# Who makes the low parts of the experts' weights: VectorE alone instead of VectorE and GpSimd in turn

## The reference

```python
for layer in range(2):
    h = h + hybrid_mixer(rmsnorm(h, attn_norm[layer]), w_in[layer], ..., w_out[layer])
    m = rmsnorm(h, ffn_norm[layer])
    h = h + (swiglu(m, ...) if layer == 0 else moe_swiglu(m, router_w[0], wg, wu, wd))
out = rmsnorm(h, final_norm)

def swiglu(h, wg, wu, wd): return (silu(h @ wg) * (h @ wu)) @ wd
# moe: y += gates[:, e:e+1] * swiglu(tokens, wg[e], wu[e], wd[e]), gates 0 but for the top two
```

## Time and profile before

| | |
|---|---|
| median of three runs | 2504.07 us |
| span of the profiled execution (its own time: no other is shown) | 2505.5 us |
| TensorE matmul busy | 2370.1 us, 95% |
| VectorE busy | 1644.0 us, 66% |
| ScalarE busy | 1241.1 us, 50% |
| GpSimd busy | 844.9 us, 34% |

### The profile page before, as it was taken

One profiled execution on the slowest core, in us unless ns is written; L12 is line 12 of the kernel. 1 busy time (PEld: TensorE's weight loads), 2 busy tenths in 40 slices (PEclk: granted clock), 3 DMA queues, 4 the chain that ended last, 5 costly groups with the idle time before them and its releaser, 6 DMA issues.

```text
span 2505.5 us, 30578 instructions
## 1 busy us (share of the span) xinstructions
PE 2370.1 (95%) x10817; PEld 1921.7 (77%) x10817; DVE 1644.0 (66%) x1608; ACT 1241.1 (50%) x1506; POOL 844.9 (34%) x354
## 2 busy tenths in 40 slices
PE   7999999999999999999999999997989889889887
PEld 6888887888888888888788878885667667667665
DVE  3457566655565655656536667666887787877877
ACT  4445444544444444444544544354566556556555
POOL 1212121121222122222112221123666666665664
PEclk9999999999999999999999999997999999999998
DMA  6454554556655555655454455542777877877877
GB/s 222 148 173 147 170 168 147 187 171 200 194 189 186 190 195 185 200 185 186 163 163 160 151 168 168 168 168 99 271 268 259 277 254 263 273 251 265 274 261 251
DMA packets 256824, 502.38 MB, mean 201 GB/s; under 512 B 13972, under 2 KB 14072, under 8 KB 256248
## 3 DMA queue, kind: packets, MB, share of 16 engines
q1 hardware_dynamic: 250368, 501.25, 60.4%
q10 hardware_dynamic: 6392, 0.25, 0.1%
HBM read 499.37 MB, written 2.10 MB: 200 GB/s over the span
## 4 chain that ended last, share of the span: by engine, by line
PE 77%; issue 7%; POOL 6%; DVE 6%; ACT 3%; DMA 0%; POOLq 0%; ACTq 0%; DVEq 0%; SPq 0%
PE acc L1303 19%; PE acc L1305 19%; PE acc L1304 19%; POOL w_lo L486 6%; PE acc L1576 4%; PE acc L1577 4%; PE acc L1578 4%; PE X L1565 2%; ACT w_hi L526 2%; DVE w_lo L810 2%; PE X L1411 1%; PE acc L1637 1%; PE X L1320 0%; PE acc L1638 0%; PE X L1331 0%
## 5 line engine op out<-in xcount | busy, mean ns | idle before, releaser
L486 POOL TENSOR_TENSOR w_lo<-raw,w_hi 128x1024 fp32r<-128x1024 f32 x331 | 830.0, 2510 | 1627.5 <-ACT w_hi L526 1176.3
L526 ACT ACTIVATE w_hi<-raw 128x1024 fp32r<-128x1024 f32 x939 | 985.4, 1059 | 754.1 <-PE acc L1305 558.0
L810 DVE TENSOR_TENSOR w_lo<-raw,w_hi 128x1024 fp32r<-128x1024 f32 x608 | 933.1, 1543 | 609.8 <-ACT w_hi L526 609.4
L1303 PE MATMUL acc<-w_hi,a_hi 128*128 128x512 f32 x1600 | 632.9, 396 | 7.7 <-POOL w_lo L486 3.7
L1305 PE MATMUL acc<-w_hi,a_lo 128*128 128x512 f32 x1600 | 625.8, 391 | 0.0
L1304 PE MATMUL acc<-w_lo,a_hi 128*128 128x512 f32 x1600 | 625.6, 391 | 0.0
L1576 PE MATMUL acc<-w_hi,a_hi 128*128 128x512 f32 x768 | 324.0, 422 | 69.0 <-POOL w_lo L486 53.8
L1303 PEld LDWEIGHTS acc<-w_hi,a_hi 128*128 128x128 f32 x1600 | 302.1, 189 | 72.4 <-issue 5.9
L1305 PEld LDWEIGHTS acc<-w_hi,a_lo 128*128 128x128 f32 x1600 | 301.8, 189 | 64.1
L1304 PEld LDWEIGHTS acc<-w_lo,a_hi 128*128 128x128 f32 x1600 | 302.2, 189 | 60.6
L1577 PE MATMUL acc<-w_lo,a_hi 128*128 128x512 f32 x768 | 309.2, 403 | 0.0
(11 more groups left out here) (222 smaller groups left out, 1627.0 us busy)
## 6 DMA issues: line engine op xcount, KB each, us to landing
raw<-in_w_in SPq DMA_DIRECT2D x112, 1024.0 KB, 5.1
raw<-in_moe_w_gate SPq DMA_DIRECT2D x68, 1024.0 KB, 5.1
raw<-in_moe_w_up SPq DMA_DIRECT2D x64, 1024.0 KB, 5.1
raw<-in_moe_w_down SPq DMA_DIRECT2D x64, 1024.0 KB, 5.1
raw<-in_dense_w_gate SPq DMA_DIRECT2D x44, 1024.0 KB, 5.2
raw<-in_dense_w_up SPq DMA_DIRECT2D x44, 1024.0 KB, 5.1
raw<-in_dense_w_down SPq DMA_DIRECT2D x44, 1024.0 KB, 5.1
raw<-in_w_out SPq DMA_DIRECT2D x32, 1024.0 KB, 5.1
```

Source lines behind the costliest of these rows:

```text
L486: nc.gpsimd.tensor_tensor(w_lo[:, u % SPLIT_SLOTS], raw[:, (u // TILE_UNITS) % RAW_SLOTS, u % TILE_UNITS], w_hi[:, u % SPLIT_SLOTS].bitcas ...
L526: nc.scalar.activation(w_hi[:, slot], raw[:, tile % RAW_SLOTS, u % TILE_UNITS], ACT.Copy)\
L810: nc.vector.tensor_tensor(w_lo[:, slot], raw[:, (u // TILE_UNITS) % RAW_SLOTS, u % TILE_UNITS], w_hi[:, slot].bitcast(F32), ALU.subtract). ...
L1303: nc.tensor.matmul(dst, hi, w_hi[:, slot, c], start=first and c == 0, stop=False)
```

## The change

GpSimd no longer makes low parts among the experts; VectorE makes all of them. `pools` is false from `M0` on, `low_ready` counts only `lo_ready` there, and GpSimd's loop and its one low part ahead of it are gone. VectorE's `picked_low` is gone too; ScalarE copies the low half right behind the high half in `picked_high`.

```diff
         def pools(u):
-            return u % 2 == 1 if u >= M0 else u % 4 == POOL_UNIT
+            return u < M0 and u % 4 == POOL_UNIT
         def low_ready(eng, u, per=0, i=None):
             if u >= M0:
-                if pools(u):
-                    eng.wait_ge(pool_ready, lin(M0 // 4 + (u - M0) // 2 + 1, per // 2, i))
-                else:
-                    eng.wait_ge(lo_ready, lin(3 * M0 // 4 + (u - M0) // 2 + 1, per // 2, i))
+                eng.wait_ge(lo_ready, lin(3 * M0 // 4 + u - M0 + 1, per, i))
@@ GpSimd
-            low_parts(M0 + 1, 0, None)
...
-            pool.wait_ge(table_ready, 1)
-            passes = pool.value_load(table[0:1, TABLE:TABLE + 1], min_val=EXPERTS, max_val=MAX_PASSES)
-            with pool.Fori(0, passes * (PASS_UNITS // 8)) as i:
-                for n in range(3, 11, 2):
-                    low_parts(M0 + n, 8, i)
@@ ScalarE, picked_high
+                nc.scalar.activation(x_lo[:, n % 4 * 4:n % 4 * 4 + 4].rearrange("p c n -> p (c n)"),
+                                     X[:, 3 - 2 * (n % 2)], ACT.Copy).then_inc(picked_lo, 1)
@@ VectorE
-            def picked_low(n, per=0, i=None):
-                dve.wait_ge(picked_ps, lin(n + 1, per, i))
-                nc.vector.tensor_copy(x_lo[:, n % 4 * 4:n % 4 * 4 + 4].rearrange("p c n -> p (c n)"),
-                                      X[:, 3 - 2 * (n % 2)]).then_inc(picked_lo, 1)
...
-            for n in range(4):
-                picked_low(n)
...
-                    if u in pick_at:
-                        picked_low(4 + pick_at[u], 4, i)
```

## The result

The changed kernel takes 2418.9 us in the median (2417.5 to 2421.4), the kernel before 2504.2 beside it: a ratio of 0.966, 95% interval 0.965 to 0.967, 85 us less. The forecast was 2458 with a range of 2424 to 2485.

What follows compares the result with a forecast made beforehand. Alternating VectorE and GpSimd low parts were taken to set the pace. A pass of 51.4 + 34.6 + 1.7 + 0.8 = 88.5 us against 95.1 gave 53 us over eight, less 7, about 46: 2458 us, range 2424 to 2485.

Steps and rivals of the forecast that it cites:

- the copies at nothing: Low-half copies moved to ScalarE: no cost taken, cover 0.6 us; uncovered at most 2.4 us a pass.
- I take 1.18 of VectorE's time each: VectorE's low parts among the experts: 1.18 us each, 48 a pass making 56.6 us; ends 1.155 and 2.06.
- the granted clock of 0.50 at the turn: Where one pass follows another: TensorE's half clock stays, spacing some eight products 0.43 instead of 0.23, 1.7 us a pass.
- about 0.1 for each of some eight restarts: TensorE restarting after pauses in a pass: some eight restarts, 0.8 us a pass added.
- The second part, 34.6: The 16 down units of a pass: TensorE leads, units, picks, putting products and small terms sum to 34.6 us, from 36.9.
- Of this I give back 7: Whole run: 7 us of the 53 us gain returned for VectorE waits a sum doesn't see, under 1 a pass.
- Rival A: TensorE's floor reached: first part 47 us, pass 83, time 2408 us; chance 0.12 together with halfway.
- halfway: Midway from forecast towards Rival A: pass 85 us, time 2424 us; chance 0.12 together with Rival A.
- Rival B: One VectorE queue replaces two, idle time stays 20 us: pass 98.7 us, slower at 2533 us; chance 0.07.
- C: Weight loads become the bound: at 275 GB/s sustained a pass needs 91.5 us, time 2475 us; chance 0.07.
- D: Low parts among experts stay 2.06 us without GpSimd: 121 us VectorE work a pass, 2712 us; chance 0.01.
- E: First part's gain lost again, for instance in ScalarE's copies and down-unit waits: within 7.5 us of now; chance 0.05.

Runs made afterwards that it cites:

- Number 6: Changed kernel plus one GpSimd subtraction of unused 128x1024 tiles at every second expert unit, nobody waiting for it: 2727.9 us, ratio 1.088.
- numbers 1 and 2: 1: changed kernel, copies of picked low halves kept on VectorE, 2418.3 us. 2: kernel before, only those copies moved to ScalarE, 2508.4 against 2506.5 us.
- number 3: Kernel before, but in a pass's last unit VectorE makes the output's low part before the weight's: 2484.4 us, ratio 0.993.
- numbers 8 and 9: Changed kernel plus one VectorE subtraction of unused 128x1024 tiles per pass, at unit 4 (8): 2418.7 us; at unit 18 (9): 2429.5 us.
- numbers 4 and 5: Changed kernel plus a VectorE instruction on unused tiles before each pass's last output low part: subtraction (4), 2426.7 us; longer reciprocal (5), 2446.6 us.
- number 10: Changed kernel with the gate's denominator and reciprocals moved from VectorE to ScalarE as exp(-ln(1 + exp(-x))): 2387.4 us, ratio 0.953.
- number 7: Changed kernel plus two GpSimd zero fills of unused 128x1024 tiles, after a tiny subtraction, at every second expert unit: 2438.7 us, ratio 0.973.

## Why the prediction was right and wrong

*What bounds, and the mechanism: right.* The two engines' turns set the pace. Number 6 shows the exclusion by itself, without any semaphore between the two; numbers 1 and 2 that the low parts are the whole of the gain. Some 22 of the 85 us are the wait at the turn with its half clocks, if they count here as in number 3, where they went without touching GpSimd; the other 63 are the pace of the low parts. The unshared lengths (0.41 and 0.27 forecast, 0.42 and 0.28 measured) and the copies at nothing hold. That GpSimd's own wait for VectorE's low part had no share of its own was not tried.

*The places: right.* TensorE leads at first, VectorE with the low parts of units 11 to 31, TensorE in the second part; numbers 8 and 9 show it by one added instruction at unit 4 and at unit 18, and the 52.4 us of waits by where they stand.

*The size: wrong by a factor of nearly two.* The forecast came to 88.5 us a pass and 89.4 with what was given back; it is 84.1. The steps that failed are the three additions to the sum, the half clock, the restarts and what was given back, 3.4 us a pass in all, for which the runs show nothing; and two terms of the sum that were sized too large. By terms:

- **"I take 1.18 of VectorE's time each"**: 1.13. I had halved a merged row of two (2.35), which holds the overlap of the last one's end. 21 of them took 23.6 us, not 24.8. VectorE's other work there takes 0.5 less too; 0.3 of waiting in front of unit 11 and a last unit of 1.8 instead of 1.4 take 0.7 back. The first part as a whole is 50.4 instead of 51.4, 1.0 less.
- **"for what I cannot remove with reason: the granted clock of 0.50 at the turn", 1.7**: it is gone, and this is the largest single error, made against my own text, which had just said that the wait ahead of it should nearly go. Number 3 shows that without this wait the kernel before loses its half clocks too, 2.8 us a pass for a wait of 1.4; so about half of that is the clock. The price was right: where the half clock stayed, in numbers 4 and 5, it cost 1.6. What decides about it is not settled: numbers 4 and 5 put the pause back, and the clock fell at one turn of seven and at four of seven.
- **"about 0.1 for each of some eight restarts", 0.8**: 0. In the first part VectorE's sum already contains TensorE's pauses, and a restart inside them delays nobody; in the second there is no pause left (33.69 of 33.70 us busy). It was counted twice.
- **The second part, 34.6**: 33.7. A pick costs 1.89 from its first load to the next unit's (below), not 2.05, the sum of two merged rows. Picks and putting products together take 11.3 instead of 11.9. Of the 0.4 for a late start next to nothing shows.
- **"Of this I give back 7"**: 0.9 a pass with no row behind it. VectorE's waits that were to fill it don't appear; it is idle 84.1 - 76.3 = 7.8 us a pass, less than the forecast's 10.

```profile
2042.60 1.08 PEld L1547 LDWEIGHTS X<-pick,o_hi 128*128 128x128 f32 x8
2043.60 0.97 PEld L1547 LDWEIGHTS X<-pick,o_lo 128*128 128x128 f32 x8
2044.49 0.19 PEld L1558 LDWEIGHTS acc<-w_hi,a_hi 128*128 128x128 f32 x1
```

Together 1.0 + 1.7 + 0.8 + 0.9 + 0.9 = 5.3 us a pass, or 42 us, which is the whole difference within 3 us. All five go the same way: every doubt was booked as a cost. Rival A (83 a pass, "halfway" 85) is the case that came nearest, though its parts, 47 and 34.6, add up to 81.6 and not to 83, and for another reason than its own: VectorE's lateness is not hidden, as the 52.4 us of waits and number 9 show. Rival B (one queue in place of two) fails: VectorE's idle time fell from 20 to 7.8 us a pass, and its waits for high parts from 113.4 us to 55.0, as the text against it had said; C was not met at 297 GB/s, but waits for loads begin in number 10 at 313 (14 of them in the row above, 1.6 us at the most); D and E are refuted by the length of a low part and the pass.

## What to carry to other kernels

Before counting two engines as two workers, look for a duration that ends one unshared length after the other engine's end; where there is one, moving the work to the faster of the two can shorten both. Price an instruction by the distance of starts in a row of its kind, not by its duration or by a merged row divided by its count. When a sum by engine gives who leads where, a pause, a restart or a half clock of the engine that doesn't lead costs nothing, and must not be added to it. Where it does lead, as TensorE at the turn, a half clock has its price (1.6 us here).

## What the runs showed of the hardware that I had not expected

- The half clock: pauses of 1.4 us are followed by it at six of seven turns of the kernel before, and without them no stretch of 0.50 stood among the experts (number 3); a pause of 1.3 or 2.6 us at the same place of a kernel with fewer other pauses brought it back at one, and at four, of seven turns (numbers 4 and 5).
- GpSimd's zero fills (0.95 us each) leave two-input subtractions of VectorE alone (largest 1.227 us) and its reciprocals (1.74), and stretch its one-input comparisons of 128 columns from 0.34 to 1.2 us in the median (number 7).
- Without any dependence, 24 subtractions of GpSimd a pass made it 38 us longer (number 6), 1.6 us for each of 2.4.
